# Spreading the first half's last step over twice as many chunks of the second up-projection, with up to four fetch buffers for x1

## The reference, cut to what matters

```python
x1 = x + gate1 * rmsnorm(merged @ w_out, g_post1)
h  = rmsnorm(x1, g_pre2) * (1 + scale2) + shift2
up = h @ w_ffn_up                      # (B, T, 2*D_FF), D_MODEL 2048, D_FF 6144
upc = causal_dwconv(ffn_buf, up, w_ffn_conv, b_ffn_conv)   # width 3
gt, val = split(upc, 2)
f  = gelu(gt) * val
y  = x1 + gate2 * rmsnorm(f @ w_ffn_down, g_post2)
```

## Time and profile before

| | |
|---|---|
| median of 3 runs | 2338.44 us (2338.01 to 2340.0) |
| profiled execution, its own time | 2340.07 us |
| its slowest core's span | 2338.0 us (core 3) |
| the page and most rows below: core 5 | span 2337.3 us |
| PE busy in the span of core 5 | 2094.1 us (90%) |
| DVE busy | 1027.5 us (44%) |
| ACT busy | 894.8 us (38%) |
| DMA queues' packets, weights / others | 67.0% / 7.9% of the 16 engines' time |

### The profile page before, as it was taken

The page is one execution under the profiler, slowest core; times in us unless marked ns, Lnnn a source line. Parts: engine busy times, 40 slices in busy tenths (PEclk is TensorE's granted clock), DMA queues, the critical chain, the costliest instruction groups (busy, mean ns, idle before and its releaser), DMA issues.

```text
span 2337.3 us, 37485 instructions; the slowest of 8 cores (2307.7 to 2338.0 us)
## 1 busy us (share of the span) xinstructions
PE 2094.1 (90%) x14624; PEld 1025.7 (44%) x14624; DVE 1027.5 (44%) x2122; ACT 894.8 (38%) x1232; POOL 146.5 (6%) x281
## 2 busy tenths in 40 slices
PE   0348989897999999999899999999999898999995
PEld 0124444443445545555445555555554343444442
DVE  0346889997521111111246666642001676665003
ACT  1357877886310000002365455441103334443111
POOL 0000000000000000000000000000000000000000
PEclk9969999998999999999999999999999999999998
DMA  7996565555355676568899987768787997889983
GB/s 173 257 199 114 93 104 103 108 96 116 69 113 101 110 126 108 106 110 160 183 196 184 183 147 142 134 125 179 133 133 129 200 205 145 149 151 182 220 163 101
DMA packets 64743, 336.06 MB, mean 144 GB/s; under 512 B 7216, under 2 KB 7728, under 8 KB 32048
## 3 DMA queue, kind: packets, MB, share of 16 engines
q0 software_dynamic: 39888, 273.17, 67.0%
q1 hardware_dynamic: 24672, 60.40, 7.9%
HBM read 585.58 MB, written 21.12 MB: 260 GB/s over the span
## 4 chain that ended last, share of the span: by engine, by line
PE 79%; DMA 7%; ACT 7%; DVE 4%; issue 2%; another core or an unknown queue 1%; SPq 0%; DVEq 0%; ACTq 0%; POOLq 0%
PE ps_all L264 79%; ACT sb_R L241 5%; DMA sb_R<-x1s 4%; DVE sb_R L244 3%; DMA sb_R<-xp 2%; ACT L241 1%; DVE sb_R L247 1%; DMA sb_w<-w_in 0%; SPq L279 0%; ACT sb_rstd L241 0%; DVE sb_mod L254 0%; DVE sb_stl L247 0%; DVE sb_R L258 0%; SPq L287 0%
## 5 line engine op out<-in xcount | busy, mean ns | idle before, releaser
L264 PE MATMUL ps_all<-sb_R,sb_w 128*128 128x512 bf16 (+2 forms) x12288 | 1926.4, 319 | 34.8 <-ACT sb_R L241 33.1
L264 PEld LDWEIGHTS ps_all<-sb_R,sb_w 128*128 128x128 bf16 x12288 | 927.5, 98 | 1014.5 <-issue 61.1
L241 ACT ACTIVATE sb_R<-ps_all 128x128 f32<-128x128 f32 (+6 forms) x416 | 206.9, 531 | 626.9 <-PE ps_all L264 464.5
L247 DVE SCALAR_TENSOR_TENSOR sb_R<-sb_R,sb_cvec 128x384 f32<-128x384 f32 (+3 forms) x576 | 369.6, 689 | 30.4 <-ACT sb_R L241 19.6
L244 DVE TENSOR_TENSOR sb_R<-sb_R 128x579 bf16<-128x579 f32 (+9 forms) x148 | 160.5, 1084 | 179.1 <-ACT sb_R L241 125.6
L241 ACT ACTIVATE sb_R<-sb_R 128x512 f32<-128x512 f32 (+9 forms) x216 | 203.3, 963 | 92.1 <-DMA sb_R<-xp 57.1
L241 ACT ACTIVATE sb_wsm<-ps_all 128x579 bf16<-128x579 f32 (+1 forms) x64 | 40.0, 625 | 398.2 <-PE ps_all L264 398.2
L241 ACT ACTIVATE sb_R<-ps_all,sb_cvec 128x579 f32<-128x579 f32 (+4 forms) x184 | 166.3, 905 | 18.8 <-DVE sb_R L244 12.9
L264 PE MATMUL ps_all<-sb_R,sb_ones 128*128 128x512 bf16 (+1 forms) x144 | 43.3, 413 | 119.3 <-ACT sb_R L241 119.3
L244 DVE TENSOR_TENSOR sb_R<-sb_R,sb_mod 128x128 f32<-128x128 f32 x96 | 27.0, 291 | 267.4 <-ACT sb_R L241 263.7
L244 DVE TENSOR_TENSOR sb_R<-sb_R,sb_rstd 128x579 f32<-128x579 f32 (+5 forms) x128 | 116.3, 934 | 22.4 <-ACT sb_rstd L241 22.4
(11 more groups left out here) (48 smaller groups left out, 707.3 us busy)
## 6 DMA issues: line engine op xcount, KB each, us to landing
sb_w<-w_ffn_up POOLq DMA_DIRECT2D x96, 1024.0 KB, 10.9
sb_w<-w_ada POOLq DMA_DIRECT2D x48, 1024.0 KB, 13.4
sb_w<-w_ffn_down POOLq DMA_DIRECT2D x48, 1024.0 KB, 10.1
sb_w<-w_in POOLq DMA_DIRECT2D x36, 1024.0 KB, 10.0
sb_w<-w_out POOLq DMA_DIRECT2D x16, 1024.0 KB, 10.8
sb_R<-xm SPq DMA_DIRECT2D x4, 2182.0 KB, 62.2
sb_R<-xp SPq DMA_DIRECT2D x4, 2170.0 KB, 51.1
sb_w<-w_lru_up POOLq DMA_DIRECT2D x8, 1024.0 KB, 12.2
```

Of the source, the lines that this page charges most:

```text
L241: return self.P.op("act", lambda e: e.activation(out=out, in_=in_, func=func, **kw), after)
L247: return self.P.op("dve", lambda e: e.scalar_tensor_tensor(out=out, in0=in0, scalar=scalar, in1=in1, op0=op0, op1=op1), after)
L264: return self.P.op("pe", lambda e: e.matmul(out, lhsT=lhsT, rhs=rhs, start=start, stop=stop), after, signal)
```

## The change

`finishA` is now advanced only in even jf, so rstd is still in jf 0 and the chunks come in jf 2, 4, ... 32. The number of x1 fetch buffers becomes NX1, the smaller of 4 and what fits between `O_X1ST` and `O_H2B`, with a semaphore each; that many fetches are issued ahead, and chunk k issues the fetch for chunk k + NX1.

```diff
+    NX1 = min(4, (O_H2B - O_X1ST) // (4 * SB_))
...
-    assert O_X1ST + 2 * 4 * SB_ <= O_H2B and O_X1B + 16 * 4 * SB_ <= O_FLO
+    assert NX1 >= 2 and O_X1B + 16 * 4 * SB_ <= O_FLO
...
-        x1s = [self.f32(O_X1ST + i * 4 * SB_, SB_) for i in range(2)]
-        x1_sem = [self.named_sem("x1s%d" % i) for i in range(2)]
-        x1_cnt = [0] * 2
+        x1s = [self.f32(O_X1ST + i * 4 * SB_, SB_) for i in range(NX1)]
+        x1_sem = [self.named_sem("x1s%d" % i) for i in range(NX1)]
+        x1_cnt = [0] * NX1
...
-            i = k % 2
+            i = k % NX1
...
-        for k in range(2):
+        for k in range(NX1):
             fetchA(k, None)
-        fA = finishA(lambda k: x1s[k % 2][:, 0:NA], lambda k: x1_tk[k],
-                     lambda k, done: fetchA(k + 2, done) if k + 2 < DK else None)
-        ftB = ffn_up("B", Ring([0, 2, 4]), fA, lambda jf: 1, [halves["A"]["pe_dn"]])
+        fA = finishA(lambda k: x1s[k % NX1][:, 0:NA], lambda k: x1_tk[k],
+                     lambda k, done: fetchA(k + NX1, done) if k + NX1 < DK else None)
+        ftB = ffn_up("B", Ring([0, 2, 4]), fA, lambda jf: 1 - jf % 2, [halves["A"]["pe_dn"]])
```

More of the change, by code:

```diff
@@ L54, in set_role @@
     global O_GB, O_GB3, O_MERGED, O_OA, O_OB, O_H2A, O_H2B, NXST, O_XST, O_FLO, O_FHI, FU, O_FU0, O_D, O_STF
-    global O_X1ST, O_X1B
+    global O_X1ST, O_X1B, NX1
     ROLE = role
```

## The result

The changed kernel took 2318.88 us in the median of 4 runs (2315.44 to 2322.2), the kernel before 2338.23 us (2334.47 to 2340.0). The ratio is 0.9912 with a 95% interval of 0.99 to 0.9924: faster by 0.9%, where 2316.2 us was forecast. In some executions of any of the kernels the cores of one die show a lower granted clock and end some per cent later; the medians here are over all executions, the ratios and intervals over the others alone. Run again beside the experiments, on two chips, the changed kernel gave 0.9917 (0.9903 to 0.9931) and 0.9906 (0.989 to 0.9921). Lines of the changed kernel's trace stand one higher than before: L265 is every matmul, L242 every ACT operation, L245 `Vtt`, L1399 the x1 fetches.

The account below looks back on a forecast made before the run. Odd cores set the time, stalled by late x1 fetches in the second up-projection. Slowest span 2338.0 - 22.2 = 2315.8 us, plus 2.07 around it, less 1.63 to the median, gave 2316.2 us; range 2313 to 2324.

Parts of the forecast that it names:

- What bounds the kernel, and the size of the stall: Second up-projection, odd cores: TensorE stalls behind DVE's wait for x1; core 5 lost 21.9 us over an unstalled 352.5.
- part 4: DMA in the second up-projection: demand falls from 238 to 195 GB/s against 197 moved; weights stay in time, cost 0.
- Part 1, the spread: Second up-projection: one chunk every second jf; DVE's work fits, last chunk ends well before the down-projection, cost 0.
- Part 2, the buffers: x1 fetches: three buffers on odd cores, two on even; 41 us to land, whole 39.9 us DVE wait gone.
- Part 3, the third fetch ahead: SP queue before the saved convolution state's load: 1.5 us more, taken as 0, at worst one weight load late.
- another stage moving by more than 3 us: Sign of being wrong altogether: even cores or a stage other than the second up-projection move by over 3 us.
- The sum: Slowest odd-core span 2338.0 - 22.2 = 2315.8 us; even cores stay at about 2310; median 2316.2 us.
- the last step, from the profiled execution to the median: Whole kernel: the profiled execution was 1.63 us over the runs' median, so 2317.9 became 2316.2 us.
- A, late weights: Second up-projection: weight landings pass 16.6 us beside x1 and y transfers; about 2352 us, chance 0.04.
- B, a rest of the stall: Second up-projection: each of 16 chunks still costs TensorE 0.6 us, so 10 us stay; 2326 us, chance 0.05.
- C, no change: x1 fetches: landing grows with the spacing, or another holder of the buffers appears; 2338 us, chance 0.03.

Follow-up runs that it names:

- the one-buffer kernel's first run: Changed kernel with a single x1 fetch buffer on every core, chunk still every second jf: 2337.89 us, ratio 0.9983 to the kernel before.

## Why the prediction was right, point by point

*What bounds the kernel, and the size of the stall.* Right. The rows gave 352.5 us for the stage without stalls, and 352.48 to 352.49 was measured on all four odd cores. The clock's part of the loss (6.6 of 21.9 us on core 5) went with the waits. Why the wait for x1 arises is under part 4.

*Part 1, the spread.* Right, and it is the whole of the gain: 0.992 alone against 0.9917 with the buffers. I had left open which part does it; spread and time to land stood as one.

*Part 2, the buffers.* The counts (3 and 2) and the time to land were right; that the third buffer matters was not claimed and is not so beside the spread. Alone it gives 0.51% of the 0.83%.

*Part 3, the third fetch ahead.* Took nothing visible: the odd cores' stage began between 1783.8 and 1788.1 us, before between 1783.6 and 1787.5. Core by core the starts did move: core 7 began 4.5 us later and core 5 3.4 us earlier. I had written that another stage moving by more than 3 us would show me wrong altogether. That sign was set too tight, since core 3 of the changed kernel alone began at 1784.7, 1791.4 and 1785.9 us in its three profiled executions.

*Part 4, the DMA load.* Right in that the load makes the fetches late: with a chunk per jf the longest landing was 24.1 to 25.8 us with two buffers and 32.4 to 34.0 with three, with a chunk every second jf and two or three buffers 13.8 to 20.9, and without the y stores the stall was gone. Weight landings fell by about 1 us in the median, and the longest stayed below the 16.6 allowed. That their lateness follows from the demand being above what was moved is argued, and one sum does not bear it out. At the 198 to 203 GB/s that cores 3, 5 and 7 moved between 1801 and 1913 us, the 1.64 MB of a jf with a chunk take 8.1 to 8.3 us, 1.2 to 1.4 more than its matmuls, and sixteen of them give 19 to 22 us, near the 21.9 to 22.4 that these cores lost. But core 1 moved 201 and lost 14.7, and the same sum for the third buffer alone, at 205 to 210 GB/s, gives 14 to 17 us where 7.4 to 10.4 were lost. So the rate is not the whole account. The store just ahead of each fetch is likely one piece that it leaves out; how far fetches sent ahead or emptier moments made up the rest was not measured.

*The sum.* 2315.8 us for the slowest span, 2316.5 measured. The median came 2.7 us above the forecast. Of this 0.7 us are that span, and the time around it was 0.5 us less than taken. The other 2.5 us are the last step, from the profiled execution to the median: I took 1.63 us off, and the median was 0.86 above. One execution is a poor guide here. With the stall gone the latest of four starts of the stage sets the time, and leaving out the chip of the one-buffer kernel's first run these starts lay between 1782.8 and 1792.6 us in the profiles. The slowest span of the four executions was 2313.9 to 2320.7 us.

*Rivals.* A, late weights: not seen; the time asked was 16.6 us and the longest landing after the change, over the three profiles of it, 16.0. The margin was thin, as the rows said; before, cores 3 and 7 had one of 16.7 us, and TensorE still did not wait. By the turn-taking rule of the Trainium skill ("DMA: Bandwidth & Descriptors", "Queues, rings and completion order") queues share each DMA engine packet by packet. The rows fit with that, in that without the y stores both became faster on core 5: weights 11.4 us in the median between 1801 and 1913 us, 13.1 with the stores, and x1 10.8 against 14.4. They do not show the turns themselves. B, a rest of the stall: none. C, no change: excluded by the first profile. The new wait that came closest to undoing the gain, the last y store ahead of the down-projection, was in part 1 at cost 0, which it is at jf 32; there I had it on DVE's work, and it is ACT's copy that waits. It takes over when the last chunk passes the up-projection's end.

## What to carry to other kernels

A fetch that is late by a little each time is first a question of how much else is asked of the DMA engines in that stretch: add up the bytes per step, divide by the step's length, and compare with what the engines move when full. Where the sum is above it, spreading the work helped more here than a further buffer: the buffer gives the fetches time but leaves the demand. The mean rate is a first guide only; what else is issued just ahead of a fetch may count too. Spread only so far that the last store is done before the next stage waits for it; one chunk too many gave back 11 to 12 us on each odd core. And look at which stores the next stage is made to wait for.

## What the runs showed of the hardware

After a wait of 2.34 us TensorE's granted clock fell to 0.60 over four microseconds, and 32 matmuls took 8.75 instead of 7.07 us; over the stage the waits cost 1.4 times their length on core 5 (21.9 / 15.3 us), and 1.1 (2.1 / 2.0 us, core 3 with one buffer) to 1.75 times (4.7 / 2.7 us, core 1 with one buffer) elsewhere. But not every wait of that size is followed by a slower clock. In the kernel with the third buffer alone, on core 1:

```profile
1865.87 7.07 PE L265 MATMUL ps_all<-sb_R,sb_w 128*128 128x512 bf16 x32 [3.08 <-ACT sb_R L242]
1875.73 7.07 PE L265 MATMUL ps_all<-sb_R,sb_w 128*128 128x512 bf16 x32 [2.80 <-ACT sb_R L242]
```

In the changed kernel's three profiled executions the odd cores went through the whole stage at the pace of a granted clock of 1.00. On the chip of the one-buffer kernel's first run, core 1 fell to 0.82 for about 5 us at a time, with no wait ahead of it. The Trainium skill, "TensorE: Matmul & The Clock Gate", section "Seeing it yourself", has a limiter that takes a die to 13/16 of the clock once three of its cores run dense matmuls, and holds it while the load lasts. The 0.82 is near 13/16; that it holds through the load is not what these rows show: core 1 was back at 1.00 from 1861 to 1873 us with TensorE busy throughout, and the changed kernel's stage ran at 1.00 on all odd cores.
